# Joints between sub-layers: order of squares, residuals and weight splits, scaling of x, transposes, and the first two column tiles together

## The chip, the cores and the metric

One NeuronCore of a Trainium2 chip. The metric is device time of one execution in microseconds (us), the median of several runs. Before the change it is 2696.19 us (3 runs: 2703.63, 2693.93, 2696.19).

## The reference

A decoder trunk of two layers over 256 tokens of width 2048, all in float32. Each layer has two sub-layers, and each of them is wrapped in the same frame:

```
mod = silu(c) @ w_ada[l] + b_ada[l]         # 6 rows of 2048: shift, scale, gate, twice
h = rmsnorm(x, g_pre) * (1 + scale) + shift
y = mixer(h)   or   conv_ffn(h)
x = x + gate * rmsnorm(y, g_post)
```

The mixer has one input projection (2048 to 5152 columns), three head groups (mLSTM, S5, sparse attention) and the output projection w_out. The second sub-layer is a gated MLP: 2048 to 2 x 5504 columns, a causal convolution of width 3, GELU times the other branch, and 5504 to 2048. `rmsnorm` is over the 2048 columns of a token. The modulation needs all 12288 columns of w_ada in each layer.

## The kernel before, in words

**Products in split precision.** TensorE multiplies pairs of rounded float32. Each operand is split in a high part and the rest: for weights ACT copies a chunk of the ring to `w_hi` (`w_head`, L1031 to 1038), and DVE subtracts to get `w_lo` (`w_rest`, L1501; helper L1406). A chunk is 128x1024, half of one column tile's (or one row tile's) weights. Chunks come from memory by SP into a ring of 5 slots; `w_hi` and `w_lo` have 4 slots (SPLIT = 4). ACT's `w_head(c)` waits until PE has counted `w_used` for chunk c - 4; DVE's `w_rest` frees the ring slot. Four chunks are split ahead (AHEAD = 4).

**Column-wise products** (input projection, `proj` L605, products L616; the MLP's first half, `wide_proj` L969, products L981 and L982). h is kept transposed in `hT`, high and low parts; an output tile is 128 columns by 256 tokens, and takes two chunks. In the up phase a unit of five k has ten column tiles, and up to six units in layer 0 and two in layer 1 carry a modulation unit: DVE's `ada_chunk` (L1412 on ada_acc, 128x1024) four times for k = 0 to 3, PE's `reduce_unit` (L590) at the end.

**Row-wise products** (w_out and the MLP's second half, `to_tokens`, L631). The output is by tokens: two token tiles t = 0, 1 of 128 tokens, 4 banks of PSUM each, all 8 banks in use. The last two row tiles are done by `last_to_tokens` (L648): all of t = 0 first, then t = 1, and `w_used` is counted in t = 1 only. The activations are split too: `x_head` on ACT (L1045), `x_rest` on DVE (L1406, x_lo).

**A joint** is what stands between a row-wise product and the next column-wise one. There are three in the program, and a start and an end that have parts of it. In order:
- ACT: the last four `w_head`s where the joint is in mid-layer (in the passage between layers there are none before the squares), then `rms` (L1047): square with sum of the product in PSUM for both token tiles, root; then the same for the new x (`rms(2)`, or `rms(0)` of the next layer).
- DVE: `residual` (L1512): per token tile the product times the gate row (L1406, 128x2048, from PSUM), the reciprocal, and x += (L1412, xs).
- PE: `reduce_unit` twice into bank 0 after the first residual; DVE copies these modulation columns out (L1847).
- DVE: `norm_in` (L1483): modA, then per token tile the reciprocal and a diagonal matrix `r_diag` (L1409, 128x128).
- PE: `norm_transposes` (L593): x of each 128x128 block times the diagonal, which scales and transposes it (L599).
- ACT `h_evac` (L1062): evacuates the banks to `hT_hi` with modulation, in eight groups b of two k; for groups 2, 5 and 7 also `h_t`. DVE does `h_t` for the others (L1409) and subtracts to `hT_lo` (L1406, hT), signal `h_lo`.
- PE: the first column tile waits for `h_lo` group by group. In mid-layer its weights are split already. At the start of a layer ACT splits four chunks before `h_evac`, and DVE's four `w_rest` stand behind all of `norm_in`.

Each engine works its own list in the order in which the program gives it, so what waits holds up all that is behind it. POOL issues the loads of w_ada, SP those of the ring. In layer 1's start SP also keeps x in memory (x_kept) once both residuals are done.

## Time and profile before

| | |
|---|---|
| median of 3 runs | 2696.19 us |
| profiled execution | 2703.81 us, span 2702.0 us |
| mean granted clock of TensorE | 0.957 of full speed |
| busy: PE, DVE, ACT, POOL | 91%, 74%, 47%, 11% |
| chain of waits that ended last | PE 73%, DVE 16%, DMA 5%, ACT 3%, issue 3% |
| memory | 643 MB moved, mean 238 GB/s |

The page comes from one profiled execution. "Busy" is the time in which an engine works on instructions. The chain of waits goes back from the last instruction to what released it. The granted clock is 1.00 at 2.4 GHz and 0.50 at 1.2 GHz.

### The profile page before, as it was taken

The page shows a single profiled execution, that of the slowest core. Times are in us where ns is not written, and L with a number is a line of the kernel's source. Part 1 is how long each engine was busy: PE and PEld are TensorE (multiplying, and loading weights), DVE is VectorE, ACT ScalarE, POOL GpSimd, SP SyncE. Part 2 cuts the span into 40 slices and gives each one's busy share as a digit, 9 for nine tenths or more (in the row PEclk, how much of TensorE's full clock was granted, in tenths as well). Part 3 has the DMA queues.
Part 4 walks back from the last instruction along what each step waited for, and adds up shares of the span by engine and source line. Part 5 has one row for each costly group of instructions (what it writes and reads, how often), then busy time and mean ns, then how long its engine had stood idle before and what let it go on. Part 6 is the DMA issues. An engine that isn't in the chain of part 4 may idle for free.

```text
span 2702.0 us, 41350 instructions
## 1 busy us (share of the span) xinstructions
PE 2452.4 (91%) x14516; PEld 2170.6 (80%) x14516; DVE 1992.8 (74%) x2383; ACT 1280.3 (47%) x1981; POOL 294.2 (11%) x434
## 2 busy tenths in 40 slices
PE   1499989888999999999998999987899999999998
PEld 1499878766888888878878999876788888887886
DVE  8788988677899996656666978767788666665555
ACT  1265455334544444444447446543454554554443
POOL 1031321111111110001001212001111000000000
PEclk9999899788999999999999999988899999999999
DMA  9648876566799996567763686545768555555554
GB/s 396 249 156 301 301 253 236 184 254 252 265 336 333 328 331 235 192 203 272 267 243 125 236 277 239 178 161 202 290 244 322 189 190 190 188 190 174 191 192 154
DMA packets 191466, 643.11 MB, mean 238 GB/s; under 512 B 28480, under 2 KB 36688, under 8 KB 189424
## 3 DMA queue, kind: packets, MB, share of 16 engines
q1 hardware_dynamic: 123520, 455.96, 47.8%
q0 software_dynamic: 47216, 170.80, 18.0%
q10 hardware_dynamic: 20608, 14.72, 1.7%
q8 instruction: 77, 1.26, 0.2%
q14 instruction: 45, 0.37, 0.0%
HBM read 626.68 MB, written 14.71 MB: 237 GB/s over the span
## 4 chain that ended last, share of the span: by engine, by line
PE 73%; DVE 16%; DMA 5%; ACT 3%; issue 3%; ACTq 0%; DVEq 0%; SPq 0%; POOLq 0%
PE ps L981 23%; PE ps L631 19%; PE ps L982 12%; PE ps L616 9%; DVE ada_acc L1412 5%; DVE w_lo L1406 3%; DVE mix L1406 3%; DMA ring<-stream 2%; PE ps L590 1%; PE ps L648 1%; ACT w_hi L1038 1%; PE ps L599 1%; PE ps L748 1%; DVE mix L1409 1%; DVE hT L1406 1%
## 5 line engine op out<-in xcount | busy, mean ns | idle before, releaser
L1406 DVE TENSOR_TENSOR w_lo<-ring,w_hi 128x1024 fp32r<-128x1024 f32 x744 | 917.6, 1239 | 518.8 <-ACT w_hi L1038 516.6
L1038 ACT ACTIVATE w_hi<-ring 128x1024 fp32r<-128x1024 f32 x744 | 787.5, 1059 | 978.7 <-PE ps L982 374.3
L981 PE MATMUL ps<-hT,w_hi 128*128 128x512 f32 x2752 | 958.7, 395 | 4.8 <-DVE hT L1406 4.8
L982 PE MATMUL ps<-hT,w_lo 128*128 128x256 f32 x2752 | 764.4, 278 | 0.0
L981 PEld LDWEIGHTS ps<-hT,w_hi 128*128 128x128 f32 x2752 | 516.3, 188 | 127.6 <-DVE hT L1406 5.3
L616 PE MATMUL ps<-hT,w_hi 128*128 128x256 f32 x2624 | 504.6, 294 | 28.6 <-DVE w_lo L1406 28.0
L982 PEld LDWEIGHTS ps<-hT,w_lo 128*128 128x128 f32 x2752 | 517.5, 188 | 0.0
L1412 DVE SCALAR_TENSOR_TENSOR ada_acc<-ada_w,cs,ada_acc 128x1024 f32<-128x1024 f32 x348 | 445.6, 1281 | 18.5 <-DMA ada_w<-ada_d 4.5
L616 PEld LDWEIGHTS ps<-hT,w_hi 128*128 128x128 f32 x2624 | 426.6, 200 | 39.3 <-issue 19.3
L616 PE MATMUL ps<-hT,w_lo 128*128 128x256 f32 x1312 | 380.2, 290 | 0.0
L631 PE MATMUL ps<-w_hi,x_hi 128*128 128x512 f32 x880 | 275.7, 395 | 23.1 <-DVE x_lo L1406 14.4
L631 PE MATMUL ps<-w_lo,x_hi 128*128 128x512 f32 x880 | 274.4, 393 | 0.0
L631 PE MATMUL ps<-w_hi,x_lo 128*128 128x512 f32 x880 | 273.6, 393 | 0.0
L616 PEld LDWEIGHTS ps<-hT,w_lo 128*128 128x128 f32 x1312 | 261.5, 199 | 0.0
L631 PEld LDWEIGHTS ps<-w_hi,x_hi 128*128 128x128 f32 x880 | 167.2, 191 | 62.0 <-DVE x_lo L1406 18.3
L505 POOL DMA_DIRECT2D ada_w<-ada_d x224 | 118.3, 529 | 881.7 <-DVE ada_acc L1412 859.1
L631 PEld LDWEIGHTS ps<-w_lo,x_hi 128*128 128x128 f32 x880 | 167.7, 191 | 35.3
L631 PEld LDWEIGHTS ps<-w_hi,x_lo 128*128 128x128 f32 x880 | 167.1, 190 | 35.1
L590 PE MATMUL ps<-cst,ada_acc 128*128 128x1 f32 x384 | 59.0, 285 | 106.4 <-DVE ada_acc L1412 88.7
L590 PEld LDWEIGHTS ps<-cst,ada_acc 128*128 128x128 f32 x384 | 58.8, 242 | 110.3 <-issue 90.8
L1353 ACT ACTIVATE mix<-ff_a,aux 128x256 f32 (+1 forms) x86 | 50.9, 592 | 89.6 <-DVE ff_a L1406 89.6
L1412 DVE SCALAR_TENSOR_TENSOR mix<-ff_a,aux,mix 128x255 f32 (+3 forms) x172 | 82.7, 481 | 14.5 <-DVE mix L1412 12.2
(231 smaller groups left out, 2008.6 us busy)
## 6 DMA issues: line engine op xcount, KB each, us to landing
ring<-stream SPq DMA_DIRECT2D x760, 512.0 KB, 4.4
ada_w<-ada_d POOLq DMA_DIRECT2D x320, 512.0 KB, 5.6
ring<-ada_d SPq DMA_DIRECT2D x36, 512.0 KB, 9.7
ada_w<-ada_d SPq DMA_DIRECT2D x28, 512.0 KB, 9.9
xs<-x SPq DMA_DIRECT2D x2, 2048.0 KB, 12.1
s_in_w<-mix ACTq DMA_DIRECT2D x8, 512.0 KB, 3.0
s_out_w<-mix ACTq DMA_DIRECT2D x16, 256.0 KB, 6.1
ring<-s_in_w SPq DMA_DIRECT2D x8, 512.0 KB, 5.8
```

Of the source, the lines that this page charges most:

```text
L505: pool.dma_start(ada_w[:, s, :], ada_d[bass.ds(u * UCH + j, 1), :, :].rearrange("a p n -> p (a n)")).then_inc(ada_full[s], 16)
L590: m = pe.matmul(ps[:, bank, col + k:col + k + 1], ada_acc[:, a, k * P:(k + 1) * P], ones[:, 0:1], start=True, stop=True)
L599: m = pe.matmul(ps[:, b, k * SEQ + t * P:k * SEQ + (t + 1) * P], xs[:, t, (2 * b + k) * P:(2 * b + k + 1) * P], r_diag[:, t, :], start=Tru ...
L616: m = pe.matmul(ps[:, bank, 0:SEQ], w[:, s, ks], h[:, k, :], start=k == 0 and p == 0, stop=k == KT - 1 and p == 2)
L631: m = pe.matmul(ps[:, 4 * t + 2 * half + b, :], xx[:, xs_, ts_], w[:, s, b * 512:(b + 1) * 512], start=k == 0 and p == 0, stop=False)
L648: m = pe.matmul(ps[:, 4 * t + 2 * half + b, :], xx[:, (k + j) % 2, ts_], w[:, s, b * 512:(b + 1) * 512], start=False, stop=j == 1 and p == 2)
L981: pe.matmul(ps[:, bank, :], w_hi[:, s, ks], hT[:, k, :, :], start=k == 0, stop=False)
L982: m = pe.matmul(ps[:, bank, SEQ:2 * SEQ], w_lo[:, s, ks], hT_hi[:, k, :], start=False, stop=k == KT - 1)
L1038: s.activation(w_hi[:, c % SPLIT, :], ring[:, at % RING, :], ACT.Copy).then_inc(hi_ready, 1)
L1353: s.activation(mtile(t), ff_a[:, k % 2, :], ACT.Identity, scale=w, bias=b).then_inc(ff_tap, 1)
L1406: return v.tensor_tensor(o, a, b, op)
L1412: return v.scalar_tensor_tensor(o, a, s, b, op0, op1)
```

## The change

The squares, residuals and the first splits of the next phase are interleaved in one order for all three joints (`joint`, on ACT and DVE). x is scaled by its reciprocal root into a buffer `xn`, in four parts per token tile, and PE transposes `xn` with true transposes. Three of the four first `w_rest` come before `norm_in`, the fourth stands in front of its third group. The first two column tiles of both column-wise products are multiplied together, group of h by group of h (`first_proj`, `first_up`); `w_used` is counted once when the first half of tile 0 is done, once when its second half is, and twice at the end. The last x_lo of a row-wise product goes between the last two splits. `o_gated` is one buffer for both token tiles, elsewhere in `mix`. The first unit of the up loop is written out. The diff, without changed signatures and repeated lines:

```diff
-        r_diag = mix[:, 2 * KT:2 * KT + TT, 0:P]
-        o_gated = mix[:, 0:KT, :].rearrange("p a b -> p (a b)").rearrange("p (t d) -> p t d", t=TT)
+        xn = mix[:, 0:KT, :].rearrange("p a b -> p (a b)").rearrange("p (t d) -> p t d", t=TT)
+        o_gated = mix[:, 2 * KT:2 * KT + 8, :].rearrange("p a b -> p (a b)")
@@ -593,24 +594,40 @@
                 for t in range(TT):
-                    diag_ready.wait(pe, l, 2 * n + t + 1)
                     for b in range(8):
+                        if b % (8 // XN_PARTS) == 0:
+                            xn_ready.wait(pe, l, (2 * n + t) * XN_PARTS + b * XN_PARTS // 8 + 1)
                         for k in range(2):
-                            m = pe.matmul(ps[:, b, k * SEQ + t * P:k * SEQ + (t + 1) * P],
-                                          xs[:, t, (2 * b + k) * P:(2 * b + k + 1) * P], r_diag[:, t, :],
-                                          start=True, stop=True)
+                            m = pe.transpose(ps[:, b, k * SEQ + t * P:k * SEQ + (t + 1) * P],
+                                             xn[:, t, (2 * b + k) * P:(2 * b + k + 1) * P], ident)
-            def proj(l, c, bank, h_part):
+            def first_proj(l):
+                for half in range(2):
+                    for b in range(4 * half, 4 * half + 4):
+                        for n in range(2):
+                            if b == 4 * half:
+                                split_ready(l * NS + (2 + half if n else half))
+                            if n or b == 0:
+                                h_lo.wait(pe, l, min(b + n + 1, 8))
+                            for k in (2 * b, 2 * b + 1):
+                                ks = slice(k % KH * P, (k % KH + 1) * P)
+                                for p, (w, h) in enumerate(((w_hi, hT_hi), (w_hi, hT_lo), (w_lo, hT_hi))):
+                                    m = pe.matmul(ps[:, n, 0:SEQ], w[:, 2 * n + half, ks], h[:, k, :],
+                                                  start=k == 0 and p == 0, stop=k == KT - 1 and p == 2)
+                            if b % 4 == 3 and n == 0:
+                                m.then_inc(w_used, 1)
+                m.then_inc(w_used, 2)
@@ -849,7 +866,10 @@
                             in_ev.wait(pe, l, n - 1)
-                    proj(l, 2 * n, n % 2, n == 0)
+                    if n == 0:
+                        first_proj(l)
+                    elif n >= 2:
+                        proj(l, 2 * n, n % 2)
@@ -966,7 +986,28 @@
-                def wide_proj(n, c, bank, free, h_part):
+                def first_up():
+                    for half in range(2):
+                        for b in range(4 * half, 4 * half + 4):
+                            for n in range(2):
+                                if b == 4 * half:
+                                    split_ready(l * NS + S_UP + (2 + half if n else half))
+                                if b == 0:
+                                    pe.wait_ge(ff_sum, l * (FREE + 2 * FT) + n + 1)
+                                if n or b == 0:
+                                    h_lo.wait(pe, l, 8 + min(b + n + 1, 8))
+                                s = (S_UP + 2 * n + half) % SPLIT
+                                for k in (2 * b, 2 * b + 1):
+                                    ks = slice(k % KH * P, (k % KH + 1) * P)
+                                    pe.matmul(ps[:, n, :], w_hi[:, s, ks], hT[:, k, :, :], start=k == 0, stop=False)
+                                    m = pe.matmul(ps[:, n, SEQ:2 * SEQ], w_lo[:, s, ks], hT_hi[:, k, :],
+                                                  start=False, stop=k == KT - 1)
+                                if b % 4 == 3 and n == 0:
+                                    m.then_inc(w_used, 1)
+                    m.then_inc(w_used, 2)
...
+                first_up()
+                for k in range(1, 5):
+                    up(0, k)
+                reduce_unit(U_UP[l], 0, U_UP[l])
+                with pe.Fori(1, N_UP[l]) as i:
@@ -1044,20 +1087,35 @@
+                def rms(n, t, l=l):
+                    if n % 2 == 0:
+                        if n or l:
+                            x_ready.wait(s, l, n - 2 + t + 1)
+                        src = xs[:, t, :]
+                    else:
+                        if t == 0:
+                            first_done.wait(s, l, n // 2 + 1)
+                        else:
+                            s.wait_ge(w_used, l * NS + (S_UP if n == 1 else NS))
+                        src = psf[:, t * D:(t + 1) * D]
+                    rms_act.by(s.activation(junk[:, t, :], src, ACT.Square, accum_out=stat[:, t:t + 1]))
+                    rms_act.wait(s, l, 2 * n + t + 1)
+                    rstd.by(s.activation(stat[:, 2 + t:3 + t], stat[:, t:t + 1], ACT.Sqrt, bias=K("eps"),
+                                         scale=1.0 / D))
+                def joint(n, l, c):
+                    rms(2 * n + 1, 0)
+                    if c is not None:
+                        w_head(c, l=l)
+                        w_head(c + 1, l=l)
+                    rms(2 * n + 1, 1)
+                    if c is not None:
+                        rms((2 * n + 2) % 4, 0, l)
+                        w_head(c + 2, l=l)
+                        w_head(c + 3, l=l)
+                        rms((2 * n + 2) % 4, 1, l)
@@ -1081,9 +1139,11 @@
-                rms(0, lambda t: xs[:, t, :])
-                for c in range(AHEAD):
-                    w_head(c, used=False)
+                if l == 0:
+                    for t in range(TT):
+                        rms(0, t)
+                    for c in range(AHEAD):
+                        w_head(c, used=False)
@@ -1325,16 +1385,17 @@
                     x_head(k, k)
-                for k in range(KT):
+                for k in range(KT - 2):
                     w_head(c)
+                    if k == KT - 3:
+                        x_head(k + 2, k + 2, l * NS + S_OUT + 2 * k + 2)
                     w_head(c + 1)
-                    if k + 2 < KT:
+                    if k < KT - 3:
-                rms(1, lambda t: psf[:, t * D:(t + 1) * D])
-                rms(2, lambda t: xs[:, t, :])
+                joint(0, l, S_UP)
...
@@ -1386,19 +1447,20 @@
+                def down(i, k, last=False):
+                    w_head(c, i)
+                    if last:
+                        x_head(k, i * 10 + (k + 2), l * NS + i * BODY + (S_DOWN + 2 * k + 2))
+                    w_head(c + 1, i)
...
+                down(4, 0, True)
                 gate_spread(1)
-                rms(3, lambda t: psf[:, t * D:(t + 1) * D])
+                joint(1, l + 1, 0 if l < DEPTH - 1 else None)
@@ -1480,15 +1542,23 @@
-                def norm_in(n, gain):
+                def scaled(n, t, l=l):
+                    rstd.wait(v, l, 4 * n + t + 1)
+                    dve.by(v.reciprocal(stat[:, 4 + t:5 + t], stat[:, 2 + t:3 + t]))
+                    v.wait_ge(dve.sem, dve.given)
+                    for i in range(XN_PARTS):
+                        part = slice(i * D // XN_PARTS, (i + 1) * D // XN_PARTS)
+                        xn_ready.by(ts(xn[:, t, part], xs[:, t, part], stat[:, 4 + t:5 + t], None, ALU.mult, ALU.bypass))
+                def norm_gain(n, gain, l=l):
                     modA_ready.by(stt(modA[:, :], modw(n + 1)[:, 2, :], 1.0, A(gain), ALU.add, ALU.mult))
-                    for t in range(TT):
-                        rstd.wait(v, l, 4 * n + t + 1)
-                        step(v.reciprocal(stat[:, 4 + t:5 + t], stat[:, 2 + t:3 + t]))
-                        diag_ready.by(ts(r_diag[:, t, :], ident, stat[:, 4 + t:5 + t], None, ALU.mult, ALU.bypass))
+                def norm_in(n, c):
                     for b in range(8):
+                        if b == 2:
+                            w_rest(c + 3)
@@ -1509,26 +1579,46 @@
+                def residual(n, t):
+                    if t == 0:
+                        v.wait_ge(gt_in, (2 * l + n + 1) * 16)
+                        if n == 0:
+                            v.wait_ge(x_back, l * 16 + 16)
+                    rms_act.wait(v, l, 4 * n + 2 + t + 1)
+                    step(tt(o_gated, psf[:, t * D:(t + 1) * D], gt_row[:, :], ALU.mult))
+                    rstd.wait(v, l, 4 * n + 2 + t + 1)
+                    step(v.reciprocal(stat[:, 6 + t:7 + t], stat[:, 2 + t:3 + t]))
+                    x_ready.by(stt(xs[:, t, :], o_gated, stat[:, 6 + t:7 + t], xs[:, t, :], ALU.mult, ALU.add))
+                    x_ready.wait(v, l, 2 * n + t + 1)
+                def joint(n, l, c, units, at, gain):
+                    residual(n, 0)
+                    w_rest(c, l=l)
+                    residual(n, 1)
+                    scaled((n + 1) % 2, 0, l)
+                    if units is not None:
+                        v.wait_ge(ada_red, units + 2)
+                        v.tensor_copy(mod2f[:, at * UG:(at + 2) * UG], ps[:, 0, 0:2 * UG]).then_inc(mod_ready, 2)
+                    if n == 1:
+                        v.wait_ge(aux_in, l * 16 + 16)
+                    norm_gain((n + 1) % 2, gain, l)
+                    w_rest(c + 1, l=l)
+                    scaled((n + 1) % 2, 1, l)
+                    w_rest(c + 2, l=l)
-                v.wait_ge(aux_in, l * 16 + 16)
-                norm_in(0, "g_pre_mix")
-                for c in range(AHEAD):
-                    w_rest(c)
+                if l == 0:
+                    v.wait_ge(aux_in, l * 16 + 16)
+                    for t in range(TT):
+                        scaled(0, t)
+                    norm_gain(0, "g_pre_mix")
+                    for c in range(AHEAD - 1):
+                        w_rest(c)
+                norm_in(0, 0)
@@ -1833,21 +1923,21 @@
+                joint(0, l, S_UP, U_OUT[l], 4, "g_pre_ffn")
                 v.sem_inc(ff_sum, FREE)
+                norm_in(1, S_UP)
...
+                if l < DEPTH - 1:
+                    joint(1, l + 1, 0, U_DOWN[l], 0, "g_pre_mix")
+                else:
+                    for t in range(TT):
+                        residual(1, t)
```

## Rows read from the trace of the kernel before

**Rows 1.** The page, part 4: the chain that ended last, by engine.

```profile
PE 73%; DVE 16%; DMA 5%; ACT 3%; issue 3%; ACTq 0%; DVEq 0%; SPq 0%; POOLq 0%
```

**Rows 2.** PE's waits, whole span: us in total, times, longest.

```profile
PE ps L616 <- DVE w_lo L1406: 28.0, 4, 9.3
...
PE ps L590 <- DVE xs L1412: 17.7, 3, 8.1
...
PE ps L631 <- issue: 8.7, 2, 4.3
```

**Rows 3.** Timeline at B: start, length, work [idle before, what ended it].

```profile
648.46 2.29 DVE L1406 TENSOR_TENSOR mix<-ps,mix 128x2048 f32<-128x2048 f32 x1 [0.73 <-ACT mix L1057]
...
650.98 2.35 DVE L1412 SCALAR_TENSOR_TENSOR xs<-mix,stat,xs 128x2048 f32<-128x2048 f32 x1
...
653.39 6.99 PE L590 MATMUL ps<-cst,ada_acc 128*128 128x1 f32 x32 [8.07 <-DVE xs L1412]
...
658.27 1.91 ACT L1057 ACTIVATE mix<-xs 128x2048 f32<-128x2048 f32 x1 [2.58 <-DVE xs L1412]
...
661.67 9.89 PE L599 MATMUL ps<-mix,xs 128*128 128x128 f32 x64 [1.30 <-DVE mix L1409]
...
668.53 1.93 ACT L1071 ACTIVATE hT<-ps,mod,modA 128x256 fp32r<-128x256 f32 x4 [7.93 <-PE ps L599]
```

**Rows 4.** Timeline, the end of w_out in layer 0.

```profile
634.12 2.35 DVE L1406 TENSOR_TENSOR w_lo<-ring,w_hi 128x1024 fp32r<-128x1024 f32 x2
...
636.86 0.73 PE L648 MATMUL ps<-w_hi,x_hi 128*128 128x512 f32 x2 [1.59 <-DVE x_lo L1406]
```

**Rows 5.** Timeline of the up phase, layer 0.

```profile
686.48 1.06 ACT L1038 ACTIVATE w_hi<-ring 128x1024 fp32r<-128x1024 f32 x1 [1.22 <-PE ps L982]
...
689.05 5.44 DVE L1412 SCALAR_TENSOR_TENSOR ada_acc<-ada_w,cs,ada_acc 128x1024 f32<-128x1024 f32 x4
...
718.04 1.22 DVE L1406 TENSOR_TENSOR w_lo<-ring,w_hi 128x1024 fp32r<-128x1024 f32 x1
...
721.92 0.40 PE L981 MATMUL ps<-hT,w_hi 128*128 128x512 f32 x1
...
727.47 0.39 PE L981 MATMUL ps<-hT,w_hi 128*128 128x512 f32 x1
```

**Rows 6.** C: timeline, and last the chain in order of time (start, length).

```profile
1401.57 1.88 ACT L1057 ACTIVATE mix<-ps 128x2048 f32<-128x2048 f32 x1 [4.43 <-PE ps L648]
...
1416.98 9.43 PE L599 MATMUL ps<-mix,xs 128*128 128x128 f32 x64 [3.65 <-DVE mix L1409]
...
1435.75 14.40 PE ps L616 x96
```

**Rows 7.** A: timeline, and last the chain in order of time.

```profile
107.56 1.06 ACT L1038 ACTIVATE w_hi<-ring 128x1024 fp32r<-128x1024 f32 x1 [0.23 <-DMA ring<-stream]
...
110.89 0.99 DVE L1409 TENSOR_SCALAR mix<-ps,modA,mod 128x256 f32<-128x256 f32 x2 [6.76 <-ACT hT L1071]
...
120.87 4.62 DVE L1406 TENSOR_TENSOR w_lo<-ring,w_hi 128x1024 fp32r<-128x1024 f32 x4
...
122.14 14.16 PE ps L616 x96
```

**Rows 8.** Groups by line: ns min/median/max; the last by form: busy us, mean ns.

```profile
L599 PE MATMUL ps<-mix,xs x256: 274/276/580, 103.8 to 1964.7; 128*128 128x128 f32 x128
L685 PE MATMUL ps<-cst,mix 128*128 128x128 f32 x64 | 8.3, 273 | 0.0
L1409 DVE TENSOR_SCALAR mix<-mix,cst x1: 352/352/352, 8.5 to 8.5; 128x256 f32<-128x256 f32 x1
L1409 DVE TENSOR_SCALAR mix<-ps,modA,mod 128x256 f32<-128x256 f32 x40 | 19.8, 536 | 28.1 <-ACT hT L1071 28.1
L1406 DVE TENSOR_TENSOR hT<-mix,hT 128x512 fp32r<-128x512 f32 x32 | 21.0, 688 | 0.7
```

**Rows 9.** Stretches: busy of PE, PEld, DVE, ACT, POOL, granted clock, DMA.

```profile
666.00:667.00 1.00, 1.00 (x7) 1.00 (x6) 0.00 (x0) 0.00 (x0) 0.00 (x0) 0.53 1.02 414
1441.00:1442.00 1.00, 1.00 (x8) 1.00 (x7) 0.00 (x0) 0.66 (x1) 0.00 (x0) 0.62 1.03 360
```

72 lines of the change are left out of this document (19 added, 53 removed).

## The prediction

> Four places are called joints here: A is the start of layer 0, B the middle of layer 0 (mixer to MLP), C the passage from layer 0 to layer 1, D the middle of layer 1. E is the end of the program.
>
> **What bounds the kernel now.** First the page's chain of waits: PE holds 73% of it and DVE 16% [rows 1]. The kernel is a stream of matmuls, so time is to be had where PE stands idle or runs slow. Then PE's own list of waits [rows 2]: 28.0 us behind the low parts of split weights in four waits, the longest 9.3 us; 17.7 us in which the sums of modulation columns wait for the residual. Other long waits stand in the mixer's middle and in the head; the change leaves them as they are. The timeline shows the places. At B, PE ends its last product at 645.3 (8.07 us before 653.39) and begins a paced first column tile only after the transposed x arrives (first evacuation 668.53) [rows 3]. At A, DVE works on h from 110.89 and only then splits four weights (4.62 us from 120.87), so the first projection starts at 122.14, long after the first part of h is there [rows 7]. C is the same: transposes at 1416.98, first projection at 1435.75 [rows 6].
>
> **The change part by part.** D has B's shape, so B is worked out and counted twice.
>
> Late x_lo. Before, the last x_lo of w_out comes behind two weight splits, and PE waits 1.6 us for it, until 636.86 [rows 4]. Now one split comes ahead and one behind. DVE's two splits run 634.12 to 636.47, so the x_lo is there at 635.7, the second split at 636.9; PE goes at 635.75 and needs the second one 6 matmul pairs, 1.36 us, later. The first token tile ends at 638.5 and the last product at 643.9: 1.1 to 1.4 us earlier.
>
> Squares, residual and scaling at B. ACT now squares tile 0 at once, not behind four w_hi. The square and its accumulator take 2.1 us (1.88 for the square [rows 6]) and start some 0.4 us after 638.5, so DVE's gated product can start at 641.0 in place of 648.46. Before, product and residual take 2.29 and 2.35 us per tile [rows 3]; one split of 1.15 us (4.62 / 4) stands between the tiles now. 641.0 + 4.85 + 1.15 + 4.85 gives 651.9 for the second residual, before 658.24. Then x of tile 0 is scaled in four parts of 128x512. No such operation is in the trace. 128x256 from SBUF with a scalar per partition took 352 ns; the same size from PSUM 536 ns [rows 8]. Per part that bounds it between 0.35 and 1.07 us; I take 0.45, nearer to the SBUF row, since both sides are in SBUF: 1.8 us a tile. PE's transposes still wait for the modulation columns to be copied out of bank 0, and this copy now stands behind the four parts: 651.9 + 0.2 + 1.8 + 0.4 = 654.4. The high end of the part would make it 656.9. The square of tile 1 and its root (from 658.27, about 2.5 us) are off the path: they lie beside the scaling of tile 0. The two w_hi moved between the squares lie beside DVE's work too.
>
> Transposes. The product with the diagonal is two instructions per 128x128 block (x256 for 128 blocks), a true transpose one (x64 for 64 blocks) [rows 8]. So the 64 instructions of a joint become 32. Before, 36 of them (tile 0 and the first pair of tile 1) took from 661.67 to 668.5. Now it is 18, and at the low clock's pace (36 in 6.86 us, mostly low, so up to 0.22 us each) they take 3.9 us. With 0.25 us for the signal the first evacuation is at 658.6, before 668.53: **9.9 us** earlier.
>
> First two tiles. DVE's part of h takes 10.0 us for eight groups (110.89 to the splits at 120.87) [rows 7], and the first h_lo comes 1.7 us in (0.99 + 0.69) [rows 7, 8]. Now one split is in front of the third group. PE has 1.38 us of work per group at full clock for two tiles (16 steps from 721.92 to 727.47 make one tile, so a pair is 11.1 us [rows 5], an eighth of it 1.38), so only the first groups are paced. Stepping through the order of first_up with h_lo at 0, 1.6, 3.4, 5.0, 6.6, 7.3, 8.9 and 9.5 us gives 12.8 us at full clock, 14.0 if the first 5.9 us run at half. Before: first matmul 671.5, second half of tile 1 used at 686.2 (the w_hi behind it starts at 686.48 [rows 5]), 14.7 us. The clock is what is open. At B it was at 1.2 GHz when the transposes began and came back to 2.4 some 5.3 us into them (the mean of 666 to 667 is 0.53); at C the projection began after 9 us of idling and the clock came back only in 1441 to 1442, 6 us into it [rows 6, 9]. Now PE idles from the end of the column sums to 654.4, then does short transposes. I take the low clock, the nearer to A and C: 14.0 us, end at 675.5, 10.7 us earlier.
>
> What is late next. The four slots of split weights now come free late: one near the end of the pair, two with its last matmul. DVE's list for the first up unit (splits, sums, taps, then four ada_acc of 1.34 us) therefore starts late: I get 681.3 for the first ada_acc, before 689.05 [rows 5], 7.75 us earlier and not 10.7. From there DVE has 11.8 us of work in a round ((718.04 - 689.05 - 5.44) / 2) where PE has 11.1, for four rounds. The slack is small: the split that ends at 719.3 is needed at 686.2 + 3 x 11.1 = 719.5 [rows 5]. So PE becomes DVE-bound there and **B and D give 7.7 us each**; 3 us of each are lost. If the clock is full, 1.2 us more each.
>
> C. There, no w_hi stood ahead of the squares. The square of tile 0 starts 0.3 us before its 1401.57; with 2.1 + 4.9 + 1.15 + 4.9 the residual of tile 1 ends at 1414.4, scaling and copy end at 1416.6, and the transposes start at 1416.8, as before (1416.98 [rows 6]). 18 transposes and the signal put the evacuation at 1420.8. The first h_lo follows at 1423.6 (1.1 us to DVE's start, 1.7 as above), and PE starts there, because three splits lie already behind it: before it started at 1435.75. The pair takes 14.2 us (0.72 us per group and tile, 5.9 us of it low; 13.0 at full clock), to 1437.8 where before it was 1435.75 + 14.40 = 1450.15 [rows 6]: **12.3 us**. DVE idles between splits for the next rounds at C, so the late slots are caught up before its long stretch, which shifts as a whole.
>
> A. Eight parts end at 107.1, three splits at 110.9, and ACT is busy with w_hi until 108.6 [rows 7]. DVE starts on h at 110.9, as it did. First h_lo 112.6, pair ends 126.8, before 122.14 + 14.16 = 136.30: **9.5 us**.
>
> E. Only the order of one x_lo: 0.3 us. More instructions on PE (the first up unit is written out) cost nothing if PE is fed in time, as in the fully written-out projections; if not, I bound it by 4.3 us a layer, PE's longest wait without a releaser in the phases touched [rows 2]. I take nothing.
>
> Sum: 9.5 + 7.7 + 12.3 + 7.7 + 0.3 = 37.5 us. The profiled execution took 2703.8 us (span 2702.0), so it would take 2666.3. The median of the runs is 7.6 us below the profiled one; the sum is taken off unchanged: 2696.2 - 37.5 = **2658.7 us**.
>
> On the clock the Trainium skill has a rule: TensorE: Matmul & The Clock Gate, Part 4: PE-mode transpose, says that the full clock does not engage for transpose-mode, which doesn't count as busy in the same way. It speaks against the true transposes. In the trace the products with the diagonal did bring the clock back at B; no row shows a long run of true transposes by themselves. By this rule the pairs start low, which is the sum above; if transposes count as those products did, the time is that of the second case below.
>
> **The rivals.**
> 1. The clock is full when the pairs begin. For it: at B the clock rose 5.3 us into the transposes [rows 9], and the new ones last some 7 us at the low pace. Against it: half as many instructions, with waits for parts. Each joint gains 1.2 us more: 2658.7 - 4.8 = 2653.9.
> 2. The backlog is larger. Slots that come free together make DVE and ACT late in the projections at A and C as well, and scaling costs 1.07 us a part. For it: DVE has its own long stretch soon after both (PE waits there already, the other two of the four waits in [rows 2]). Against: after both joints DVE idles between single splits, so a backlog has room to drain. B and D lose 2.5 us more each, C 2.5, and A and C 3 us each in the backlog: 13.5 us lost, 2672.2.
> 3. The rearranged order does not overlap: the gated product on the first banks and PE's products on the others disturb each other, or the longer code stalls PE 4.3 us a layer. At C a square of PSUM already lies beside matmuls and takes 1.88 us, as little as elsewhere [rows 6], which speaks against. With 2.5 us for every joint's slowed products and 4.3 us a layer half of the gain goes, 18.6 us: 2677.3.
> 4. The other side, slower. The pairs are paced by h and hold PE in short pieces, so the clock doesn't come back and stays at 1.2 GHz into the phases that follow. Each us of PE work so lost costs 0.5 us. It decides at 75 us of low clock over the four joints: 75 x 0.5 = 37.5. With 95 us it ends at 2658.7 + 47.5 = 2706. Against it: at C the clock rose about 6 us after steady matmuls began, in mid tile [rows 9].
>
> **How the numbers follow.** Forecast 0.42, rival 1 0.20, rival 2 0.20, rival 3 0.12, rival 4 0.03, and 0.03 for a change that does nothing measurable. The likeliest is 2658.7. The range takes in rival 1 less some 9 us, for the spread of the runs (2693.9 to 2703.6) and for scaling parts at their low end, and at the top rival 2 and nearly half of rival 3: 2645 to 2676. About 0.5%, 13.5 us, is what can be told from no change: rival 3 comes near that. Faster 0.90 (the forecast, rivals 1 and 2, and two thirds of 3), same 0.06, slower 0.04.
>
> **What would show it.** Right: the 9.3 us waits for w_lo gone from PE's list; half as many transposes; evacuations at B some 9 to 10 us after the last residual's start; x_lo waits of 1.6 us down to under 0.5; a new PE wait for w_lo of some 3 us in all in the first up unit of each layer; pair of tiles in 14 us with the low clock at its start. Wrong: a pair above 16 us, the column copy much later than 0.5 us behind the last scaled part of tile 0, parts near 1 us, or PE waiting on fetch in the first up unit.

## The result, and the profile after

The changed kernel takes 2666.9 us (median of 4 runs, 2658.1 to 2673.0), the kernel before in the same comparison 2699.6 us: a ratio of 0.9876, 95% interval [0.9853, 0.9898], so 33 us less (27 to 40). A second comparison of the same two kernels gave 0.9835 [0.9806, 0.9864], 42 us less. The forecast was 2658.7 us, a gain of 37.5. The profiled execution after took 2666.9 us against 2703.8, which is 36.9 less. The experiments show that this sum is right in part by chance: by the profiles the joints gave more than forecast, and one untouched loop took some of it back.

In the page's chain of waits PE's share falls by 2 points and DVE's rises by 3; compare [rows 1]. Then PE's list of waits after, to be read against [rows 2].

```profile
PE 71%; DVE 19%; DMA 4%; ACT 3%; issue 3%; ACTq 0%; DVEq 0%; SPq 0%; POOLq 0%
```

```profile
PE ps L648 <- DVE x_lo L1468: 16.9, 4, 7.1
PE ps L633 <- DVE w_lo L1468: 9.6, 3, 4.7
...
PE ps L601 <- DVE mod L1603: 9.1, 3, 4.0
PE ps L648 <- issue: 8.7, 2, 4.4
...
PE ps L618 <- DVE hT L1468: 5.9, 4, 2.9
PE ps L591 <- DVE xs L1474: 4.9, 3, 1.6
...
PE ps L1003 <- DVE hT L1468: 3.8, 4, 1.6
...
PE ps L1020 <- DVE w_lo L1468: 2.8, 6, 0.8
```

The 9.3 us waits for w_lo are gone (28.0 us became 9.6), and the sums of modulation columns (L591) wait 4.9 us in place of 17.7. The wait of the transposes (L601) for the column copy, 9.1 us, takes the place of a wait for the diagonal matrix in the kernel before:

```profile
PE ps L599 <- DVE mix L1409: 7.2, 4, 3.6
```

New is the wait of the first up unit (L1020) for late splits, 2.8 us in six pieces. The timeline at B, which answers to [rows 3]:

```profile
634.35 1.88 ACT L1102 ACTIVATE mix<-ps 128x2048 f32<-128x2048 f32 x1 [4.01 <-PE ps L665]
...
636.45 2.29 DVE L1468 TENSOR_TENSOR mix<-ps,mix 128x2048 f32<-128x2048 f32 x1 [2.27 <-ACT mix L1102]
...
641.38 5.64 PE L591 MATMUL ps<-cst,ada_acc 128*128 128x1 f32 x32 [1.63 <-DVE xs L1474]
...
645.02 2.35 DVE L1474 SCALAR_TENSOR_TENSOR xs<-mix,stat,xs 128x2048 f32<-128x2048 f32 x1
...
647.60 1.96 DVE L1471 TENSOR_SCALAR mix<-xs,stat 128x512 f32<-128x512 f32 x4
649.48 0.16 DVE L1603 COPY mod<-ps 128x16 f32<-128x16 f32 x1
...
649.70 5.37 PE L601 MATMUL ps<-cst,mix 128*128 128x128 f32 x32 [2.67 <-DVE mod L1603]
...
653.64 1.93 ACT L1129 ACTIVATE hT<-ps,mod,modA 128x256 fp32r<-128x256 f32 x4 [3.90 <-PE ps L601]
...
656.63 0.47 PE L1003 MATMUL ps<-hT,w_hi 128*128 128x512 f32 x1 [1.56 <-DVE hT L1468]
...
675.28 5.45 DVE L1474 SCALAR_TENSOR_TENSOR ada_acc<-ada_w,cs,ada_acc 128x1024 f32<-128x1024 f32 x4
```

ACT squares tile 0 0.2 us behind its product; the residual, the four parts and the copy follow with no gap but the split, and the transposes wait on the copy alone. The chain in order of time at A and at C (start, length), for [rows 7] and [rows 6]:

```profile
106.83 2.96 DVE w_lo L1468 x3
...
113.64 12.52 PE ps L618 x90
127.03 3.00 PE ps L633 x25
...
1400.34 4.00 PE ps L601 x18
1404.42 1.03 ACT hT L1129 x2
...
1409.04 11.65 PE ps L618 x90
1421.57 2.52 PE ps L633 x21
```

Groups by form (busy us, mean ns) for [rows 8], and the granted clock (the last but two of the columns) in the middle of B's transposes for [rows 9]:

```profile
L601 PE MATMUL ps<-cst,mix 128*128 128x128 f32 x128 | 22.5, 359 | 10.1 <-DVE mod L1603 9.1 <-DVE mix L1471 1.0
L1471 DVE TENSOR_SCALAR mix<-xs,stat 128x512 f32<-128x512 f32 x32 | 13.7, 490 | 0.3
```

```profile
652.00:654.00 2.00, 2.00 (x15) 2.00 (x14) 1.93 (x4) 0.36 (x1) 0.00 (x0) 0.72 1.01 401
```

The granted clock rose from 1.2 to 2.4 GHz at 653.1, 3.4 us into the true transposes and 3.5 us before the first product, so the pair (the first two column tiles, multiplied together) ran at 2.4 GHz.

**Where the time went, by stages.** Each number is the difference of two starts on PE's timeline, good to about 0.2 us. A runs from the start of the span. A ends, and B, C and D run from the first matmul of the last w_out or w_down block, where the third column tile's first matmul starts. "Up unit" is from there to the first column sum in the up phase, "rest of up 1" from that sum of layer 1 to w_down. "All else" ends with the last product; the 11.7 us behind it are the same in all four profiles. Both kernels were profiled twice (the second times are two of the experiments).

```
us              before        changed       forecast change
A            136.9 136.9    126.8 126.9     -9.5
B             53.8  52.9     40.9  41.9     -10.7
up unit 0     44.4  45.2     47.3  47.3     +3.0
C             55.3  55.1     41.7  41.8     -12.3
D             54.0  53.9     41.2  41.9     -10.7
up unit 1     44.4  45.2     47.3  47.3     +3.0
sum          388.8 389.2    345.2 347.3     -37.2
rest of up 1 429.6 429.6    436.7 436.7      0
all else    1871.9 1870.2  1871.5 1869.2    -0.3
```

The joints with their up units gave 42.8 us (means of two), and the rest of layer 1's up phase took 7.1. All else is as it was in sum; its parts are not that steady (the mixer of layer 0 took 416.7 and 423.3 us in the two profiles of the kernel before, 419.9 and 419.2 in those of the changed one).

### The profile page after: what moved, and what is told of

The parts are those of the page before. It is cut to its first block, busy times and chain, and to the rows that moved or that the text cites. A ratio compares the mean times of both kernels' runs of the same rounds, so it can differ in the third digit from the quotient of the medians.

```text
span 2665.1 us, 41027 instructions
## 1 busy us (share of the span) xinstructions
PE 2436.5 (91%) x14388; PEld 2150.7 (81%) x14388; DVE 2001.4 (75%) x2407; ACT 1278.0 (48%) x1981; POOL 293.1 (11%) x434
## 4 chain that ended last, share of the span: by engine, by line
PE 71%; DVE 19%; DMA 4%; ACT 3%; issue 3%; ACTq 0%; DVEq 0%; SPq 0%; POOLq 0%
PE ps L1020 22%; PE ps L648 21%; PE ps L1021 11%; PE ps L633 7%; DVE ada_acc L1474 6%; DVE w_lo L1468 4%; DVE mix L1468 3%; DMA ring<-stream 2%; PE ps L665 1%; PE ps L618 1%; PE ps L591 1%; PE ps L765 1%; DVE mix L1474 1%; DVE mix L1471 1%; ACT w_hi L1081 1%
## 5 line engine op out<-in xcount | busy, mean ns | idle before, releaser
L1020 PE MATMUL ps<-hT,w_hi 128*128 128x512 f32 x2688 | 943.6, 397 | 2.8 <-DVE w_lo L1468 2.8
L1021 PE MATMUL ps<-hT,w_lo 128*128 128x256 f32 x2688 | 750.8, 279 | 0.0
L1020 PEld LDWEIGHTS ps<-hT,w_hi 128*128 128x128 f32 x2688 | 504.6, 188 | 125.8 <-DVE w_lo L1468 4.7
L1021 PEld LDWEIGHTS ps<-hT,w_lo 128*128 128x128 f32 x2688 | 506.6, 188 | 0.0
L633 PE MATMUL ps<-hT,w_hi 128*128 128x256 f32 x2496 | 477.9, 293 | 9.6 <-DVE w_lo L1468 9.6
L633 PEld LDWEIGHTS ps<-hT,w_hi 128*128 128x128 f32 x2496 | 403.6, 199 | 20.4 <-issue 19.8
L633 PE MATMUL ps<-hT,w_lo 128*128 128x256 f32 x1248 | 360.3, 289 | 0.0
L633 PEld LDWEIGHTS ps<-hT,w_lo 128*128 128x128 f32 x1248 | 247.0, 198 | 0.0
L591 PE MATMUL ps<-cst,ada_acc 128*128 128x1 f32 x384 | 56.0, 277 | 93.5 <-DVE ada_acc L1474 88.7
L591 PEld LDWEIGHTS ps<-cst,ada_acc 128*128 128x128 f32 x384 | 55.8, 231 | 97.4 <-issue 90.8
L1474 DVE SCALAR_TENSOR_TENSOR mix<-ff_a,aux,mix 128x255 f32 (+3 forms) x172 | 82.7, 481 | 16.1 <-DVE mix L1474 13.9
```

Source lines behind the costliest of these rows:

```text
L591: m = pe.matmul(ps[:, bank, col + k:col + k + 1], ada_acc[:, a, k * P:(k + 1) * P], ones[:, 0:1], start=True, stop=True)
L633: m = pe.matmul(ps[:, bank, 0:SEQ], w[:, s, ks], h[:, k, :], start=k == 0 and p == 0, stop=k == KT - 1 and p == 2)
L1020: pe.matmul(ps[:, bank, :], w_hi[:, s, ks], hT[:, k, :, :], start=k == 0, stop=False)
L1021: m = pe.matmul(ps[:, bank, SEQ:2 * SEQ], w_lo[:, s, ks], hT_hi[:, k, :], start=False, stop=k == KT - 1)
L1474: return v.scalar_tensor_tensor(o, a, s, b, op0, op1)
```

## Experiments

Times are medians of 4 to 12 runs, with the ratio to the kernel before in the same comparison, or of a single run where that is said. Single executions of one kernel spread over 7 to 18 us (the kernel before once over 30), so edits of a few us are judged by the stages: "sum" is that of the table, 346.2 in the changed kernel (mean of 345.2 and 347.3). Each variant has one profile, and the changed kernel's two sums lie 2 us apart, so a difference of 2 us or less between sums shows nothing by itself.

**1. Tiles one after another.**

```diff
-  for half: for b in half: for n in 0, 1: (waits, two k steps)
+  for n in 0, 1: for half: for b in half: (waits for h if n == 0, two k steps)
```

> The changed kernel, but the first two column tiles are multiplied one after the other again, in the first projection and in the first up unit; splits, squares, scaling and true transposes stay. Theory (the pairing hides about half a tile of PE work behind DVE's work on h): at B the low part of the last group of h is there 8.9 us after the pair began, and tile 0 can end only 0.7 us behind it; a second tile of 5.55 us follows. That is 15.2 us for both against 12.5 us measured for the pair, 2.5 to 2.7 us a joint, at A, B, C and D, so 10 us in all: about 2677. Rival (the pairing only moves the loss, because at B and D its two weight slots come free late and DVE starts the next round late): only A and C lose 2.6 us each, B and D nothing: about 2672, and the first long DVE block of the up phase starts no later than in the changed kernel.

2666.6 us, 0.9872 [0.9847, 0.9896]. A 129.0, B 44.2, C 44.7, D 45.2, the up units 45.2 each: a sum of 353.6. The pairing is worth 2.3 to 3.7 us at each joint, 11.7 in all, and the up units give back 2.1 each: 7.5 us net, between the theory's 10 and the rival's 5. The rival's mechanism (slots freed late) is real and takes a third. The whole time doesn't show these 7.5 us: its median is that of the changed kernel (2666.9 and 2663.3), where 2677 had been expected. The worth of the pairing thus rests on the stages of one profile. PE's waits from B's first up matmul to the third tile, in this kernel and then in the changed one:

```profile
PE ps L999 <- DVE hT L1462: 4.2, 6, 0.8
```

```profile
PE ps L1003 <- DVE hT L1468: 2.3, 2, 1.6
```

**2. The old order of squares, residual and splits.**

```diff
 def joint(n, l, c):                # ACT; the same on DVE with w_rest and residual
+    if n == 0: four w_head
     rms(2n+1, 0); rms(2n+1, 1); rms(2n+2, 0); rms(2n+2, 1)   # no w_head between
+    if n == 1: four w_head         # on DVE: four w_rest behind norm_in
```

> The changed kernel, but squares, residual and weight splits stand in the order of the kernel before: at B and D four high parts and four low parts ahead of the squares and the residual, at A and C the four splits behind all of h. Pairing, scaling in four parts and true transposes stay. Theory (the order is the main part of the gain): the pair at A and C can only begin when DVE has ended h (10 us) and the first splits, some 9 us after its present start, and then runs without stalls (11.1 for 12.5 us), so 8 us each; at B and D the first evacuation comes 6.3 us later (23.2 us after the last product before, 13.9 us now, 3 us of this by the transposes) and the pair is 1 us shorter because no split lies within h, so 5.3 us each. 26.6 us in all: about 2693. Rival (transposes and pairing carry most of the gain, the order only what the waits of B show): 12 us or less, under 2679.

2693.4 us, 0.9966 [0.9951, 0.998]: the theory. A 136.7, B 46.1, C 52.2, D 46.3, sum 375.5. Taken back by itself, the order is worth 29.3 of the 42.8 us, and here the whole time agrees: it is 26 to 30 us above the changed kernel's. Its waits are back: the timeline at B and PE's list.

```profile
660.93 6.98 PE L591 MATMUL ps<-cst,ada_acc 128*128 128x1 f32 x32 [8.07 <-DVE xs L1475]
```

```profile
PE ps L618 <- DVE w_lo L1469: 22.1, 4, 10.6
```

**3. How a block is turned.** Three kernels: products of the scaled block with the identity, each true transpose issued twice, and products of the unscaled block with a diagonal as before.

```diff
-  pe.transpose(ps_block, xn_block, ident)
+  pe.matmul(ps_block, xn_block, ident, start=True, stop=True)    # products
+  pe.transpose(ps_block, xn_block, ident)   # issued two times   # twice
+  pe.matmul(ps_block, xs_block, r_diag[:, t, :], start=True, stop=True)  # diagonal
```

> The changed kernel, but each scaled block is turned by a product with the identity (two instructions a block, 64 a joint) in place of a true transpose (one, 32 a joint). Theory (true transposes save PE instructions, and the clock counts them as it counts products): tile 1's 16 blocks become 32 instructions at some 0.17 to 0.22 us, so the first evacuation comes 2 to 3 us later at B, C and D and 1 us at A: 7 to 10 us in all, about 2675; the low clock ends about as long after the first turning instruction as now (3.5 to 3.9 us), and the pair is at full clock in both. Rival 1 (only products wake the clock, and what ended the low stretch in the changed kernel was something else): the low stretch at B is clearly shorter than 10.2 us, and the loss is 1 us a joint or less. Rival 2 (DVE's work on h is the bound in any case, so a later first evacuation is caught up): under 3 us in all.

> The changed kernel, but each true transpose is issued twice, into the same place: 64 true transposes a joint, as many instructions as the 64 of the products with a diagonal or the identity. Theory (the price of a turn is its number of PE instructions, whichever kind): the joints are as long as with products (44.5, 43.8 and 42.9 us at B, C and D, 2 to 3 us over the changed kernel's), and the low clock at B ends 3 to 4 us after the first transpose, before any product. Rival (true transposes cost less than a product's pass, or don't count for the clock): the joints are under 1 us longer, or the low clock lasts until after the first product of the up unit and the pair takes 1 us or more longer than 12.5 us.

> The changed kernel, but with the old turning: x is not scaled, each block is multiplied with the diagonal matrix of the factors (64 instructions a joint). Order, pairing and x_lo stay. Theory (the count of PE's instructions decides, as in the run with products): PE starts to turn 1.7 us earlier as nothing is scaled ahead, but 36 instructions to the first evacuation take 7.0 us in place of 4.0, so the first evacuation is 1.0 to 1.5 us later at A, B, C and D, 4 to 6 us in all; true transposes and scaling together are worth that much of the change. Rival (DVE bounds the joints, and has 3.5 us less to do a joint): joints and first up units sum to 346 or less, no loss.

Products: 2670.5 us, 0.9874 [0.9853, 0.9895], sum 352.9. Twice: 2665.5 us in a single run, sum 352.0. Diagonal: 2664.6 us, 0.9853 [0.9811, 0.9895], sum 347.1. The same group of turning instructions in the three, in this order:

```profile
L601 PE MATMUL ps<-cst,mix 128*128 128x128 f32 x256 | 37.7, 321 | 10.9 <-DVE mod L1604 9.9 <-DVE mix L1472 1.0
```

```profile
L602 PE MATMUL ps<-cst,mix 128*128 128x128 f32 x256 | 36.7, 317 | 11.0 <-DVE mod L1604 10.0 <-DVE mix L1472 1.0
```

```profile
L602 PE MATMUL ps<-mix,xs 128*128 128x128 f32 x256 | 36.3, 313 | 6.2 <-DVE mod L1603 5.4 <-DVE mix L1473 0.8
```

The number of instructions sets the price, whichever kind: 64 true transposes cost what 64 product instructions cost, 6 to 7 us over the changed kernel. The means in these rows mix both levels of the clock. At one level the kinds are alike: from start to start a true transpose takes 109 ns at 2.4 GHz and 213 at 1.2, a product instruction 112 and 213. But true transposes need x scaled first. The diagonal needs no scaling, starts to turn 1.4 us sooner behind the last product at C and D, and its sum is only 0.9 us over the changed kernel's: the rival held, and "scale and transpose" against "multiply with a diagonal" is a draw within the changed kernel's own spread (345.2, 347.3). Against true transposes with the scaling in one part (343.2, see 6) the diagonal is 3.9 us behind, so a few us for the transposes are not ruled out. The second kernel shows the clock: at D it issues nothing but true transposes from 1915.63 to its first up matmul at 1924.62.

```profile
1915.60:1919.00 3.40, 3.37 (x16) 3.37 (x17) 3.35 (x8) 0.15 (x1) 1.71 (x4) 0.50 0.59 207
1919.00:1924.00 5.00, 5.00 (x47) 5.00 (x46) 2.09 (x4) 2.38 (x6) 0.00 (x0) 0.98 1.03 418
```

It rises among them, 3.6 us after the first. In the profiles of this kernel, of the one with products and in both of the changed one, the rise comes 3.4 to 5.8 us after the first turning instruction at B, C and D, products or transposes alike. Column sums (5.6 us of them at D) run ahead of the transposes, with 2.7 us of idling between; whether they help towards the rise, no run separates. In the kernel before they did not bring it by themselves: 7.0 us of them at B (653.4 to 660.4) ran at 1.2 GHz throughout, and the clock came back 5.3 us into the turning.

**4. The column copy ahead of the scaled parts, and tile 1 scaled by ACT.**

```diff
     residual(n, 1)
+    tensor_copy(mod2f ...)
     scaled(t=0)
-    tensor_copy(mod2f ...)
# second kernel, besides, at B, C and D:
-    four parts of tile 1 on DVE
+    four activations Copy, scale=stat[:, 5:6], on ACT
```

> The changed kernel, but the modulation columns are copied out of bank 0 ahead of the four scaled parts of tile 0 and not behind them, so the transposes need not wait for the copy. Theory (DVE bounds the joint: from the first residual to the last part of h it has 0.8 us of idling at B): the 2.7 us wait of PE at the transposes shrinks to 1 us or so, the first transposes come 1.5 us earlier, but those of tile 1 wait for scaled parts that stand behind a weight split, so the first evacuation moves by under 0.5 us: the time stays within 1.5 us of the changed kernel. Rival (PE's transposes bound the joint): B, C and D gain 1.5 us each, 4.5 us in all, about 2662.

> The changed kernel, but at B, C and D tile 1 is scaled by ACT (four parts of 128x512 with the reciprocal as scale) in place of DVE, the column copy stands ahead of tile 0's scaled parts, and both splits stand behind tile 1's reciprocal. Theory (DVE bounds the joint): DVE loses 1.7 us of work a joint, the first h starts up to 1.5 us earlier and the last h ends 1.7 us earlier, so B, C and D are 1.5 us shorter each, 4.5 us in all. Rival (PE's transposes and ACT's evacuations bound the joint): ACT scales until later than DVE did, its evacuations start no earlier, and the joints change by under 0.5 us.

Copy first: 2656.4 us, 0.9834 [0.9812, 0.9856], sum 344.3 (B 41.4, C 40.7, D 41.1). ACT: 2663.1 us, 0.9848 [0.9817, 0.988], sum 344.2 (B 41.3, C 40.7, D 41.1). Each is 2 us under the changed kernel, no more than its two profiles differ, and the second is no better than the first: DVE's 1.7 us less a joint bought nothing, so my theory that DVE bounds the joint fell in the second kernel, where the first evacuation comes no sooner behind the last product than with the copy moved alone (14.0 us at B and 12.8 at C in both, 13.3 for 12.5 at D) and the pair is 13.0 us as before. In the first, D shows that DVE can be the bound: the transposes start sooner, and PE then waits for a split that stands ahead of h.

```profile
1919.53 5.28 PE L601 MATMUL ps<-cst,mix 128*128 128x128 f32 x32 [3.12 <-DVE mix L1471]
1926.83 0.47 PE L1003 MATMUL ps<-hT,w_hi 128*128 128x512 f32 x1 [2.02 <-DVE hT L1468]
```

```profile
1923.84 1.22 DVE L1468 TENSOR_TENSOR w_lo<-ring,w_hi 128x1024 fp32r<-128x1024 f32 x1
1924.97 0.99 DVE L1471 TENSOR_SCALAR mix<-ps,modA,mod 128x256 f32<-128x256 f32 x2
```

The median of the first kernel is 7 to 10 us under that of the changed one, far more than its joints gave. Its profile has 429.6 us for 436.7 in the rest of layer 1's up phase, on which more in 6; the profiled execution itself took 2666.1 us, as its mixer of layer 0 was 6.6 us longer (426.5).

**5. The slots of the pair.**

```diff
+  out[:, [at + 1, at + 2]] = out[:, [at + 2, at + 1]]     # packing of the first pair
-  slot 2 * n + half, one slot freed at half, three at the end
+  slot 2 * half + n, two freed at half, two at the end    # and one split less ahead of h
```

> The changed kernel, but the second and third weight block of each first pair change places in the packed stream, so that the pair uses slots 0 and 1 in its first half and 2 and 3 in its second: the slots come free in the order in which the pair ends with them, and only two low parts have to stand ahead of h. Theory (the 3.1 us that DVE's late start costs in the first up unit come from three slots freed together): from the third tile's start to the first column sum of layer 0's up phase it takes 44.5 to 45.5 us in place of 47.5, at D too, and A is 1 us shorter: 5 to 7 us in all. Rival (DVE has too much work in that unit whatever the slots do): 47 us or more, and only A's 1 us is gained.

> The two last edits together: tile 1 scaled by ACT at B, C and D, the column copy first, and the first pair's weight blocks in the order in which the pair ends with them; with DVE's work on h relieved, only one split lies within h at B, C and D. Theory (the swap's earlier slots and ACT's scaling add up, as the pair is then no longer paced by splits within h): pairs of 13.0 us at B and D and 13.9 at A and C, 1.3 us less in the first up units, so joints and first up units sum to 341 to 342 us, against 345.2 and 347.1 in the changed kernel: 4 to 5 us faster, 2658 to 2660. Rival (the swap's gain in the first up unit is lost in the pair whatever DVE does, as in the swap alone): the sum is 344 or more, no gain.

Swap alone: 2661.5 us, 0.9831 [0.98, 0.9863]. The up units fall to 46.1 and 45.9, a gain of 1.2 to 1.4 each and short of the 2 or more I expected, and the pairs at B and D take 13.6 us in place of 13.0, as two splits now lie within h. A, for which I expected 1 us less, is 0.4 us shorter; sum 344.9. Together with the edits of 4: 2655.6 us (6 runs, 2651.7 to 2661.3), 0.9821 [0.9788, 0.9854], sum 338.0, pairs of 12.4 us at B and D, up units 45.9 and 46.3. That is 8.2 us under the changed kernel, more than the 4 to 5 expected. I read it so that with both DVE is through h sooner and the slots come in order; no run separates the two. PE's waits for w_lo in the up phase, in the changed kernel 2.8 us:

```profile
PE ps L1019 <- DVE w_lo L1472: 1.2, 3, 0.5
```

This version has the lowest median of all that were run; its interval overlaps the changed kernel's.

**6. Both kernels again, and one part in place of four.**

```diff
-XN_PARTS = 4
+XN_PARTS = 1
```

> The changed kernel once more, unchanged, for the spread of its stages. The two profiles so far agree at the joints but not between them: the mixers and up phases, which the change doesn't touch, differ by up to 10 us between profiles of kernels that have the same code there. Theory (these differences come with the execution, not with the code): A, B, C and D repeat within 0.5 us (126.7, 40.9, 41.7 and 41.2 us), and the first mixer (419.9) and the second up phase (484.0) come out several us different. Rival (they belong to the changed kernel): both repeat within 1 us, and layer 1's up phase again runs its inner matmul pairs at 353 ns instead of 346.5.

> The kernel before once more, unchanged, for the spread of its stages. In its first profile the stretches that the change does not touch (mixers, w_out but its last part, up phases from the first column sum on, down phases) sum to 2301.5 us, in nine profiles of kernels with the change to 2299.9 to 2308.3. Theory (their spread belongs to the execution): the sum falls somewhere in 2300 to 2308, by all the kernels' rows, and the joints with the first up units sum to 388.8 within 2 us. Rival (the change costs the untouched stretches some us): the sum is again under 2302.

> The changed kernel, but x of a tile is scaled in one instruction of 128x2048 and not in four of 128x512. Theory (at B, C and D the transposes of tile 0 wait for the column copy behind the scaling anyway, and those of tile 1 lie behind tile 0's): B, C and D change by under 0.6 us, and only A is later, by up to 1.3 us; one instruction takes about 1.7 to 1.9 us. Rival (the parts let PE start earlier everywhere): 1.3 us at each of the four joints.

Changed kernel again: 2663.3 us, 0.9835 [0.9806, 0.9864]. Before again: 2702.5 us in a single run. One part: 2656.9 us in a single run, sum 343.2; its scaling of 128x2048 takes 1.34 us against four times 0.49. The parts gain nothing anywhere, A included (125.5 us, where I had allowed for 1.3 us more).

The untouched stretches of the kernel before (the last two lines of the table) sum to 2299.8 this time: under 2302, as the rival said. The difference to the changed kernel's 2308.2 and 2305.9 is the rest of layer 1's up phase. The up matmul over the same 300 us of it (ns min/median/max), before, before again, changed, changed again, one part:

```profile
L981 PE MATMUL ps<-hT,w_hi x867: 391/393/396, 2119.8 to 2420.0; 128*128 128x512 f32 x174
```

```profile
L981 PE MATMUL ps<-hT,w_hi x867: 392/395/395, 2119.7 to 2419.9; 128*128 128x512 f32 x174
```

```profile
L1020 PE MATMUL ps<-hT,w_hi x850: 394/398/404, 2079.7 to 2379.7; 128*128 128x512 f32 x170
```

```profile
L1020 PE MATMUL ps<-hT,w_hi x851: 395/398/403, 2079.7 to 2380.0; 128*128 128x512 f32 x171
```

```profile
L1020 PE MATMUL ps<-hT,w_hi x867: 392/392/395, 2079.7 to 2379.9; 128*128 128x512 f32 x174
```

867 matmuls or 850 in the same time, at 2.4 GHz in all: 346 or 353 ns for a step of two. Of 14 profiles four have the slow pace in this loop (436.7 us): both of the changed kernel, the serial one and the one with products. The other ten have 429.6 to 430.7. Nor is it the chip: on one and the same chip the serial kernel and the one with products had the slow pace, those with the old order and with the copy first the fast one. Each of the two kernels repeats its own value here, which would fit a cost of the program. But the first up units speak against that: the kernel before ran 40 us of the same loop at the fast pace in its first profile and at the slow one in its second, at 2.4 GHz in both.

```profile
L981 PE MATMUL ps<-hT,w_hi x116: 392/394/396, 686.9 to 726.8; 128*128 128x512 f32 x116
```

```profile
L981 PE MATMUL ps<-hT,w_hi x114: 395/398/403, 693.2 to 733.1; 128*128 128x512 f32 x114
```

This is the whole difference of its up units, 44.4 and 45.2 us. So one program can have either pace, and eight of the twelve profiles with the new joints have the fast one in layer 1. What sets it stays open, and the 7.1 us are not shown to be a cost of the change. The mixers differ by up to 12 us (414.2 to 426.5 in layer 0), between kernels and between two profiles of one.

The earlier x_lo was not tried alone. The last block of w_out or w_down from its first matmul to its last fell from 12.5 us at B and D (12.1 in the second profile) to 10.7 and 11.0 (11.0 and 11.8): means of 1.5 us at B and 0.9 at D. PE's 1.6 us wait for x_lo [rows 4] is not in the list of the first profile after; in the second 0.8 us of it is.

## Why the prediction was right, and where it was not

**Order at B: right.** From the end of tile 0's product to the end of the second residual 13.4 us were forecast and 13.3 measured (634.1 to 647.4); to the column copy's end 2.5 and 2.3; from there to the first evacuation 4.2 and 4.0. The scaled part was taken at 0.45 us and measured 0.49. The 1.36 us for "6 matmul pairs" are those of six matmuls; nothing hangs on it.

**x_lo: right in size.** 1.1 to 1.4 us forecast, 1.5 and 0.9 measured at B and D (means of two). C gained 0.4 us from it too, which the sum left out.

**The clock: wrong.** "I take the low clock" for the start of the pairs failed. In both profiles of the changed kernel 2.4 GHz came back among the transposes, before the pair began at B, C and D, which is the first rival's mechanism, priced at 1.2 us a joint. The pair took 13.0 us (forecast 14.0, or 12.8 at full clock) at B and D, and 13.9 (14.2, or 13.0) at C. Only A's pair had 3.4 us of low clock in it, in both profiles. By the rule of the Trainium skill cited in the prediction (TensorE: Matmul & The Clock Gate, Part 4: PE-mode transpose) the full clock doesn't engage for transpose-mode; the rows of the kernel with each transpose issued twice show the opposite here.

The rows of the kernel before held the hint. The prediction took C as a case for the low clock, since the projection there began after 9 us of idling and waited 6 us for the rise. But the clock had come back at 1421.3 in C's turning too, and fell again only at 1431.5, in the gap that the pair no longer has:

```profile
1421.50:1431.00 9.50, 4.91 (x44) 4.72 (x43) 6.39 (x12) 8.44 (x18) 0.00 (x0) 1.00 0.00 0
```

**The backlog in the first up unit: right in kind, smaller in size.** 3 us were forecast at B and at D; the stage grew from 44.4 and 45.2 to 47.3. At the slow pace of the loop, which the serial kernel and the second profile of the kernel before have there (45.2), it is 2.1 us; the other 0.8 is pace. DVE's first ada_acc at B starts 10.1 us earlier than before, counted from the start of the last w_out block, where 7.75 were forecast; it lags 2.8 us behind the gain of the pair's end, for 3 forecast. The backlog disappears with serial tiles, and the swap of slots takes off 1.2 to 1.4, so freeing three slots at once is about half of it. PE's waits for w_lo there are 1.5 us in layer 0 and 1.3 in layer 1, in three pieces each, where some 3 in each layer were named as the sign.

**The sums.** A: 10.0 us for 9.5. B with its up unit: 9.5 (means of two) for 7.7, D 9.9 for 7.7; the clock gave 1.0 us and the smaller backlog 0.5 of it at each, the rest is not traced. C: 13.4 for 12.3; half of the excess is that the pair before was taken at 14.40, the chain's group of 96, where the stage to the third tile's first matmul is 15.0. Together 42.8 for 37.2. Against it stand the 7.1 us in layer 1's up loop, a loss in a stretch that I had taken to be unchanged, which no term of the sum and no rival held. So the total of 36.9 between the profiles came out at the forecast 37.5 by luck, through two errors that cancel: 5.6 us more gained at the joints than forecast, 7.1 us lost elsewhere. The chance for a larger backlog (second rival) and for no overlap (third) didn't come: the gated product took 2.29 us beside PE's products, as long as in the kernel before, where PE stood idle then [rows 3], and PE had no new wait without a releaser (8.7 us in both).

**What I credited wrongly.** The prediction read like a sum in which transposes and scaling are a good part. The runs give 29.3 us to the order, 7.5 to the pairing net of its backlog, about 1 to the turning (within the 2 us by which two profiles differ), and leave some 5, which go to x_lo (about 3 us by the lengths of the last blocks) and to what the edits share; that is worked out, not run.

## What to carry to other kernels

When DVE feeds PE at a joint, first put what the next stage waits for ahead of what fills buffers for later: taking this alone back cost two thirds of the gain, and no other part was near it. Before interleaving two tiles, look at the order in which their buffers come free, and lay out the data so that they are freed in the order of the next requests. Judge edits of a few us by stages between two marks in the trace and profile each kernel twice: a loop that the edit doesn't touch differed by 7 us between kernels here, and a mixer by 6.6 us between two profiles of one kernel.

## What the hardware showed

- A true transpose of a 128x128 fp32 block is one PE instruction where a product with the diagonal or identity is two (x128 against x256), and costs per instruction the same: from start to start 109 ns against 112 at 2.4 GHz, 213 against 213 at 1.2.
- TensorE's clock went from 1.2 to 2.4 GHz within a run of true transposes alone (0.50, then 0.98).
- The same fp32 loop ran at 346 or at 353 ns a step at the same granted clock, in different programs and, in the first up unit, in two executions of one program. The cause is open.
- An fp32 scaling of SBUF by a scalar per partition takes 1.34 us for 128x2048 in one instruction on DVE and 1.96 or 1.7 in four. On ACT a part of 128x512 takes 0.71 us:

```profile
L1123 ACT ACTIVATE mix<-xs,stat 128x512 f32<-128x512 f32 x12 | 7.7, 711 | 2.0 <-DVE stat L1553 2.0
```
